# The column sums of modulation chunks 2 to 5, issued two steps later among the value projection's products

## The reference, cut to what matters

```
sh1, sc1, gt1, sh2, sc2, gt2 = split(silu(c) @ w_ada + b_ada, 6)
hc = modulate(rmsnorm(ctx, g_pre_mix), csh1, csc1)          # 256 context tokens
pc = hc @ w_in[:, :COL_Q];   kc, vc, gfc, gbc = gla_inputs(pc)
hx = modulate(rmsnorm(x, g_pre_mix), sh1, sc1)              # 512 tokens
yx = token_mixers(hx @ w_in, states from the context, ...)   # k, v, gates, q, four branches
x  = x + gt1 * rmsnorm(yx @ w_out, g_post_mix)
x  = x + gt2 * rmsnorm(conv_ffn(modulate(rmsnorm(x, g_pre_ffn), sh2, sc2), ...), g_post_ffn)
```

## Time and profile before

| | us |
|---|---|
| median of 3 runs | 1464.11 (1462.46, 1464.11, 1471.2) |
| profiled execution, its own time | 1459.95 |
| its span in the trace | 1458.1 |
| PE busy (matmul) | 1382.9 (95%) |
| DVE busy | 891.7 (61%) |
| POOL busy | 837.2 (57%) |
| ACT busy | 398.1 (27%) |
| mean granted clock of PE | 0.975 |

### The profile page before, as it was taken

The page is one execution under the profiler, slowest core; times in us unless marked ns, Lnnn a source line. Parts: engine busy times, 40 slices in busy tenths (PEclk is TensorE's granted clock), DMA queues, the critical chain, the costliest instruction groups (busy, mean ns, idle before and its releaser), DMA issues.

```text
span 1458.1 us, 19719 instructions
## 1 busy us (share of the span) xinstructions
PE 1382.9 (95%) x6923; PEld 1115.3 (76%) x6923; DVE 891.7 (61%) x1274; ACT 398.1 (27%) x757; POOL 837.2 (57%) x651
## 2 busy tenths in 40 slices
PE   5898889989699999999999999999799999999998
PEld 4676768878378888888877888767588888888887
DVE  5676488763666666674018789745675888887000
ACT  3431223332422222211013202355423233232000
POOL 1233334425466666667775677432267777777664
PEclk9889999989899999999999999999999999999999
DMA  9356222212123333345332232211032333333332
GB/s 354 128 187 216 59 58 49 68 44 64 39 80 93 101 100 89 100 128 172 94 111 61 85 101 87 73 56 47 26 98 85 96 101 101 87 100 93 91 94 83
DMA packets 224459, 142.05 MB, mean 97 GB/s; under 512 B 5611, under 2 KB 211088, under 8 KB 224400
## 3 DMA queue, kind: packets, MB, share of 16 engines
q1 hardware_dynamic: 221333, 136.45, 31.2%
q10 hardware_dynamic: 3067, 4.78, 1.0%
HBM read 139.12 MB, written 2.10 MB: 97 GB/s over the span
## 4 chain that ended last, share of the span: by engine, by line
PE 83%; DVE 8%; issue 4%; ACT 2%; POOL 2%; DMA 0%; POOLq 0%; SPq 0%; DVEq 0%; ACTq 0%
PE ps L553 25%; PE ps L554 24%; PE ps L555 24%; PE ps L845 2%; DVE norm_acc L1698 1%; POOL w_lo L516 1%; PE ps L1088 1%; PE ps L1104 1%; PE ps L1117 1%; DVE SS L1991 1%; ACT h_hi L1198 1%; PE ps L639 1%; DVE xT L2162 1%; POOL w_hi L513 1%; DVE h_lo L1719 1%
## 5 line engine op out<-in xcount | busy, mean ns | idle before, releaser
L516 POOL TENSOR_TENSOR w_lo<-raw,w_hi 128x1024 fp32r<-128x1024 f32 x213 | 535.1, 2512 | 17.8
L553 PE MATMUL ps<-h_hi,w_hi 128*128 128x512 f32 x1064 | 427.3, 402 | 12.7 <-DVE h_lo L1719 7.1
L554 PE MATMUL ps<-h_lo,w_hi 128*128 128x512 f32 x1064 | 418.9, 394 | 0.0
L555 PE MATMUL ps<-h_hi,w_lo 128*128 128x512 f32 x1064 | 418.7, 394 | 0.0
L512 POOL TENSOR_TENSOR w_hi<-raw,cst 128x16 fp32r<-128x16 f32 x213 | 63.3, 297 | 573.6 <-PE ps L555 515.4
L553 PEld LDWEIGHTS ps<-h_hi,w_hi 128*128 128x128 f32 x1064 | 202.2, 190 | 65.9 <-issue 18.8
L555 PEld LDWEIGHTS ps<-h_hi,w_lo 128*128 128x128 f32 x1064 | 202.4, 190 | 43.5
L554 PEld LDWEIGHTS ps<-h_lo,w_hi 128*128 128x128 f32 x1064 | 202.7, 190 | 39.7
L513 POOL TENSOR_SCALAR w_hi<-raw 128x1008 fp32r<-128x1008 f32 x213 | 232.8, 1093 | 0.0
L2080 DVE SCALAR_TENSOR_TENSOR f_acc<-ps,par,f_acc 128x441 f32<-128x441 f32 (+2 forms) x176 | 122.3, 695 | 50.3 <-ACT f_acc L1198 27.9
L553 PE MATMUL ps<-f_hi,w_hi 128*128 128x512 f32 x352 | 138.4, 393 | 0.5 <-POOL w_lo L516 0.5
(11 more groups left out here) (301 smaller groups left out, 1944.3 us busy)
## 6 DMA issues: line engine op xcount, KB each, us to landing
raw<-in_w_up SPq DMA_DIRECT2D x88, 512.0 KB, 3.7
raw<-in_w_in SPq DMA_DIRECT2D x59, 512.0 KB, 3.7
raw<-in_w_down SPq DMA_DIRECT2D x32, 512.0 KB, 3.7
ada_first<-in_w_ada SPq DMA_DIRECT2D x8, 1024.0 KB, 10.2
raw<-in_w_out SPq DMA_DIRECT2D x16, 512.0 KB, 3.6
v_tok<-in_w_ada SPq DMA_DIRECT2D x14, 512.0 KB, 6.1
raw<-in_w_down SPq DMA_DIRECT2D x16, 384.0 KB, 3.3
ada<-in_w_ada SPq DMA_DIRECT2D x10, 512.0 KB, 5.4
```

Of the source, the lines that this page charges most:

```text
L516: pool.tensor_tensor(w_lo[:, slot % 2, :], raw[:, slot, :], w_hi[:, slot % 2, :].bitcast(F32), ALU.subtract).then_inc(S("lo_split"), 1)
L553: nc.tensor.matmul(dst, lhs_hi, rhs_hi, start=first, stop=False)
L554: nc.tensor.matmul(dst, lhs_hi, rhs_lo, start=False, stop=False)
L555: return nc.tensor.matmul(dst, lhs_lo, rhs_hi, start=False, stop=last)
```

## The change

`ada_sum(k)` was called in steps k = 2 to 5, for chunks 2 to 5. Now `ada_sum(k - 2)` is called in steps k = 4 to 7, for the same chunks in the same order, again behind the decay sums of its step. Nothing else in the program differs; the waits of other engines on the count `ada_out` and PE's wait on `ada_added` are the same numbers as before.

```diff
                 if 2 <= k < 8:
                     sums(k - 2)
-                if 2 <= k < 6:
-                    ada_sum(k)
+                if k >= 4:
+                    ada_sum(k - 2)
```

## The result

| | before | changed |
|---|---|---|
| median of 14 runs each, us | 1464.55 (1460.35 to 1471.2) | 1455.14 (1450.93 to 1461.86) |
| ratio | | 0.9939, 95% interval 0.9923 to 0.9955 |
| profiled execution, its span | 1459.95, 1458.1 | 1455.9, 1454.1 |
| the same kernel on two later occasions | | 0.9955 (0.9939 to 0.9972), 0.9970 (0.9952 to 0.9987) |

The change makes the kernel quicker, by 9.4 us in this comparison of medians, by 6.8 and 4.7 in the two later ones. Over all executions of this study (33 changed, 118 before, copies of either among them) the means are 1456.1 and 1462.5, 6.4 us apart; the forecast was 4.7, and the profiled spans are 4.0 apart. This is "within 1%", as forecast. The three comparisons differ by somewhat more than their intervals lead one to expect, and why is not known.

A forecast was written before the change was run, and what follows sets the result against it. TensorE (PE), 83% of the chain, was taken as the bound: 7.07 us saved on its path, less 1.7 slow clock and 0.7 DVE wait, gives 4.7 us sooner, from 1464.1 to 1459.4 us; range 1453.5 to 1466.

The forecast's parts named there:

- Step 1: Ahead of T4 (value-loop step k = 4): start stays set by unit 7's weight split, wait grows from 0.85 to about 2.8 us.
- Step 2: PE from T4 to the branch at full clock: waits and slow clock gone, branch could start at 147.20, 7.07 us sooner.
- Step 3: PE behind the wider gap ahead of T4: a half-clock stretch follows, costing 1.7 us, bounds 0 and 2.7.
- Step 4: Chunk 4's accumulation on DVE: 8.8 us, done near 137.4, wanted by T6 at 140.0; hidden, 2.6 us to spare.
- Step 5: Chunk 5's accumulation on DVE, beside unit 9's POOL split: T7's column sums wait 0.7 us, bounds 0 and 4.3.
- Step 6: SyncE's queue: unit 9's weights load later, near 135.1, but stay hidden, with 0.6 us to spare at the worst.
- Step 7: From the branch start to the end: the 7 us are carried through, give or take a slow stretch that falls elsewhere.
- Rival A: At T4 the clock stays up after the 2.8 us gap: 6.4 us sooner, 1457.7; chance 0.17.
- Rival B: Before T7's column sums and the branch, DVE's chain turns the moved wait into an equal one: no gain, 1464; chance 0.14.
- Rival C: Ahead of T7's column sums, accumulations of chunks 4 and 5 become the bound: 6.5 us later, 1470.6; chance 0.06.

The follow-up runs named there:

- early7_after: The changed kernel with unit 7's weights loaded ahead of pieces 15 and 16 instead of behind them; ratio to before 0.9976 (0.9961 to 0.9992).

## Why the prediction was right, and by how much

**The time.** Forecast 1459.4 in a range of 1453.5 to 1466, measured 1455.14: the sign and the order were right, the size about half of the first comparison and three quarters of all executions together (4.7 against 6.4). The first trace alone looks better than the forecast deserves. Its stretch is 4.7 us shorter than before's, as forecast to a tenth, but two misses of equal size cancel in it: T4 starts 0.67 us later behind T2's decay sums than forecast, and T7's column sums wait under 0.1 us instead of 0.7. That is luck.

**Step 1, the gap ahead of T4.** Right in kind: T4 still starts when unit 7's split is done. Forecast 2.8 us, measured 3.4, 2.2 and 3.0; the split itself moves by a microsecond or two with the landing of its weights (it began at 119.70, 117.51 and 119.78 in the three traces, at 118.56 in before).

**Step 2, PE's path.** Right. T5, T6 and T7 took 6.22, 6.22 and 6.30 us, as summed to within 0.06. At full clock the sum was 5.42 + 0.79 - 1.82 = 4.4 us, and the stretches of five traces without their slow clock are 4.4 us apart. The executions' 4.3 +- 0.4 in span x clock is near that but not the same quantity: 1.4 us of the stall were at half clock, half of which counts in the other row, so the sum would be 3.7 there.

**Step 3, the clock behind the wider gap.** Right in kind, and its size is open. I took 1.7 us as if it came each time. It came in two of three traces (1.6 us each: T4 in 5.92 and 5.93 us) and not in the third (4.31), a mean of 1.1. The executions do not decide it: span x (1 - clock) fell by 1.9 +- 0.8 us, and in that measure the forecast is 3.4 (half of the 6.8 us at half clock from 131.7 to 138.5 in before) less 1.7, that is 1.7; with 1.1 instead it is 2.3. The Trainium skill's sentence in "TensorE: Matmul & The Clock Gate", Part 1, weighed there, speaks of the slow matmuls at a kernel's start; the traces show that the same kernel differs from run to run in mid-kernel too, with these numbers. The term should have been a mean of both cases, not a choice of one. One of the two rows behind it was also misread. In the row of 763.40 to 766.65 the gap itself stands at 0.50: the clock had fallen by 763.2, while PE was still busy, so this fall did not follow the gap:

```profile
755.00:763.20 8.20, 8.20 (x57) 7.50 (x56) 0.51 (x3) 1.35 (x3) 7.08 (x6) 1.00 0.38 114
763.20:766.65 3.45, 0.20 (x2) 0.03 (x1) 2.99 (x5) 0.72 (x1) 0.00 (x0) 0.50 0.53 152
```

**Step 4, chunk 4.** Right: 8.6 us of DVE work (8.8 forecast), 2.65 us to spare (2.6).

**Step 5, chunk 5.** The mechanism was right (the split of unit 9 delayed DVE's last four additions by 2.8 us, forecast up to 3.65), but the wait was under 0.1 instead of 0.7 us. It is the larger of the two terms in which the traces differ from the sum. The margin is nil: 149.02 against 149.0. That it is no margin shows in early7_after, where PE came sooner and waited 3.20 us.

**Step 6, unit 9's weights.** Right: issued at 137.92, which is the forecast 135.1 plus T4's later start (1.1) and slow clock (1.6); landed in 6.4 us; 1.5 us to spare.

**Step 7, the rest.** Not contradicted. From the branch to the end nothing was gained; without slow clock the three traces of the changed kernel are 0.2 to 3.0 us longer there than the two of before, and those of all kernels here lie between 1284.8 and 1289.0, so that a loss of 1 to 2 us is neither shown nor excluded.

**Where the missing microseconds are.** The forecast's sum is 4.4 from PE's path, about 1 from the slow clock (2.6 less 1.7) and -0.7 for chunk 5. The traces have 4.4, 1.5 and under 0.1: 5.9 us in the stretch, against 6.4 in the means of all executions. How often T4 is slow in the other executions is not known, and neither is how the 9.4 us of the first comparison divide, since the clock was not listed for before there.

**Rival A** (7.07 - 0.7 = 6.4 us) describes the second trace in kind, whose stretch is 7.7 us shorter, and that its 6.4 is the mean of all executions is chance; forecast and A are not two kernels' fates but two kinds of execution of one. **Rival B's** chain through DVE is real and reached PE's path with under 0.1 us at T7. **Rival C** did not occur.

## What to carry to other kernels

When an instruction waits for another engine that itself waits for the step just before, move it far enough back that both halves of the loop fit in between, and check each instance by itself: one step was enough for chunk 4 and not for chunk 5. Moving a consumer back also holds its buffer longer; here that cost nothing only because the producer's work still ended just in time. The order with the shortest stretches left the early consumers where they were and moved the late ones; by the medians it is not shown to be better. A gain of this size should be stated as two terms, the part at full clock, which a trace's own stretch gives to a microsecond or less, and the slow clock, which needs the mean of many executions.

## What the runs showed of the hardware

- The clock after a gap is no function of its length alone: half clock followed gaps of 1.47, 2.96, 3.39 and 3.52 us ahead of T4, full clock those of 0.59 to 1.38 us and one of 2.19 us.
- Half clock can be granted while PE is idle, and costs nothing then: 16.2 of 73.7 us in before. Read as a loss, before's mean granted clock says 36.9 us where PE's work lost 28.8.
- A tiny DVE operation can take as long as POOL's big one beside it: 2.32 us (early7_after) instead of 0.15 (before) for 64x8 elements. POOL pays too where it begins during one of DVE's additions: its 128x1024 subtraction takes 2.70 us there (145.78 in the changed kernel), 2.34 alone (121.00 there), and 2.35 where it began before DVE's pair (119.86 in before).
- Filling a 5.4 us wait of PE with products kept the clock up there, and the kernel as a whole was measured 0.18% slower (0.04 to 0.31). That is one experiment; its cause is not settled.
